# Four edits at once in a two-layer attention and ConvFFN kernel: the input stage, two waits filled with products, a shorter norm step, and the second attention's outputs split ahead of the sample

## The reference, cut to what matters

```python
h = rms_norm(x, norm1)
a_q, a_k, a_v, b_q, b_k, b_v, i_q, i_k, i_w = split_cols(h @ w_in, PROJ_SPLITS)
b_q = rms_norm(b_q.reshape(B, T, N_HEADS_B, HEAD_DIM), q_norm)
b_k = rms_norm(b_k.reshape(B, T, N_HEADS_B, HEAD_DIM), k_norm)
o_a = stick_breaking(a_q, ka, va, q_pos, k_pos)
# B: every query takes the top_k keys by an indexer's score, bias by T5 bucket, softmax
o_b = indexed_sparse_attention(b_q, kb, vb, i_q, ki, i_w, q_pos, k_pos, rel_bias, top_k)
x = x + jnp.concatenate([o_a, o_b], axis=-1) @ w_out
f, conv_new = conv_ffn(rms_norm(x, norm2), conv_state, w_up, conv_w, conv_b, w_down)
return x + f, new_rows + (conv_new,)
```

## Time and profile before

| | us |
|---|---|
| median of three runs | 1620.74 |
| the profiled execution's own time | 1622.25 |
| its span, first to last instruction | 1620.5 |
| PE busy | 1551.6 (96%) |
| DVE busy | 928.3 (57%) |
| ACT busy | 684.6 (42%) |
| POOL busy | 628.4 (39%) |
| mean granted TensorE clock | 0.991 |

### The profile page before, as it was taken

The page is one execution under the profiler, slowest core; times in us unless marked ns, Lnnn a source line. Parts: engine busy times, 40 slices in busy tenths (PEclk is TensorE's granted clock), DMA queues, the critical chain, the costliest instruction groups (busy, mean ns, idle before and its releaser), DMA issues.

```text
span 1620.5 us, 29945 instructions
## 1 busy us (share of the span) xinstructions
PE 1551.6 (96%) x11838; PEld 1443.5 (89%) x11838; DVE 928.3 (57%) x1721; ACT 684.6 (42%) x1302; POOL 628.4 (39%) x346
## 2 busy tenths in 40 slices
PE   6999999989999999999999999998899999999998
PEld 5788887759999999999987898876699999999998
DVE  6666666746566156426757666666466642662461
ACT  4425564554444144224433355455434432442342
POOL 5223232326543433434542333232374434434332
PEclk9999999999999999999999999999999999999999
DMA  4444321112323223223242422211132332332323
GB/s 134 134 126 134 85 75 39 57 58 66 91 79 92 85 86 92 82 89 89 76 115 82 117 75 77 66 44 43 61 92 79 92 92 79 92 92 79 91 79 97
DMA packets 246338, 138.19 MB, mean 85 GB/s; under 512 B 11006, under 2 KB 239214, under 8 KB 246198
## 3 DMA queue, kind: packets, MB, share of 16 engines
q1 hardware_dynamic: 246198, 136.28, 29.0%
HBM read 121.19 MB, written 14.24 MB: 84 GB/s over the span
## 4 chain that ended last, share of the span: by engine, by line
PE 79%; DVE 10%; ACT 4%; issue 2%; POOL 2%; DVEq 2%; ACTq 1%; DMA 0%; SPq 0%
PE g_ps L1224 15%; PE g_ps L1225 14%; PE g_ps L1228 14%; PE a_ps L1225 8%; PE a_ps L1224 8%; PE a_ps L1228 8%; PE a_ps L709 2%; DVE prob L1697 1%; PE a_ps L1322 1%; PE a_ps L1303 1%; POOL w_lo L1721 1%; PE a_ps L1349 1%; DVE score L1639 1%; ACT w_hi L940 1%; PE a_ps L1416 1%
## 5 line engine op out<-in xcount | busy, mean ns | idle before, releaser
L1721 POOL TENSOR_TENSOR w_lo<-raw,w_hi 128x1024 fp32r<-128x1024 f32 (+2 forms) x210 | 504.3, 2402 | 698.5 <-ACT w_hi L940 698.4
L1224 PE MATMUL g_ps<-h_hi,w_hi 128*128 128x272 f32 (+1 forms) x1616 | 449.9, 296 | 10.2 <-DVEq L1598 4.1
L1225 PE MATMUL g_ps<-h_lo,w_hi 128*128 128x272 f32 (+1 forms) x1616 | 439.6, 290 | 0.0
L940 ACT ACTIVATE w_hi<-raw 128x1024 fp32r<-128x1024 f32 (+2 forms) x210 | 217.5, 1036 | 457.2 <-PE g_ps L1228 317.9
L1228 PE MATMUL g_ps<-h_hi,w_lo 128*128 128x272 f32 (+1 forms) x1616 | 337.3, 290 | 0.0
L1224 PEld LDWEIGHTS g_ps<-h_hi,w_hi 128*128 128x128 f32 (+1 forms) x1616 | 306.2, 189 | 25.0 <-issue 9.1
L1225 PEld LDWEIGHTS g_ps<-h_lo,w_hi 128*128 128x128 f32 (+1 forms) x1616 | 306.0, 189 | 0.6
L1607 DVE SCALAR_TENSOR_TENSOR wts<-work,par,wts 128x546 f32<-128x546 f32 x176 | 202.6, 1151 | 99.6 <-ACT wts L1122 92.2
L1228 PEld LDWEIGHTS g_ps<-h_hi,w_lo 128*128 128x128 f32 (+1 forms) x1616 | 254.4, 189 | 0.0
L1224 PE MATMUL a_ps<-h_hi,w_hi 128*128 128x272 f32 x720 | 194.9, 288 | 0.0
L1225 PE MATMUL a_ps<-h_lo,w_hi 128*128 128x272 f32 x720 | 194.4, 288 | 0.0
(11 more groups left out here) (233 smaller groups left out, 2718.8 us busy)
## 6 DMA issues: line engine op xcount, KB each, us to landing
raw<-in_w_up SPq DMA_DIRECT2D x88, 512.0 KB, 3.7
raw<-in_w_in SPq DMA_DIRECT2D x56, 512.0 KB, 3.6
raw<-in_w_down SPq DMA_DIRECT2D x32, 512.0 KB, 3.8
raw<-in_w_out SPq DMA_DIRECT2D x16, 512.0 KB, 3.8
raw<-in_w_down SPq DMA_DIRECT2D x16, 384.0 KB, 3.4
strip<-bias_turns SPq DMA_DIRECT2D x12, 256.0 KB, 3.5
bias_turns<-bias_line SPq DMA_DIRECT2D x8, 320.0 KB, 5.2
x_nat<-in_x_prompt SPq DMA_DIRECT2D x4, 512.0 KB, 5.7
```

Source lines behind the costliest of these rows:

```text
L940: act.activation(w_hi[:, n % SPLIT, 0:kt, 0:c], raw[:, n % RAW, 0:kt, 0:c], ACT.Copy).then_inc(hi_done, 1)
L1224: pe.matmul(g[0:c, a, 0:HALF], w_hi[:, s, j, 0:c], xh[:, mov], start=(j == 0), stop=False)
L1225: pe.matmul(g[0:c, a, 0:HALF], w_hi[:, s, j, 0:c], xl[:, mov], start=False, stop=False)
L1721: pool.tensor_tensor(w_lo[:, s, 0:kt, 0:c], raw[:, n % RAW, 0:kt, 0:c], w_hi[:, s, 0:kt, 0:c].bitcast(F32), ALU.subtract).then_inc(lo_done, 1)
```

## The change

1. **Input stage.** x is loaded by four DMAs issued from ACT's queue at the start; SP loads only identity and ones, the sample's x and the gains before the weights, and the tables and masks later. PE starts when the identity and the sample's x are there. The squares of the eight tiles are made by ACT (new step "SX", L1014) in PSUM and added by DVE. R moves between the halves of ("iq", 0), the bias line between the halves of ("iq", 1).
2. **Products in two waits.** Fourteen bf16 products of 240 columns before the sums N of ("bk", 1), 24 before BL of pair j = 12. They go to columns of a PSUM bank that nothing reads.
3. **Norm step.** ACT squares y after making it (`va` = y^2). DVE has three operations: raw * gain * y, (total + n*eps) * y^2, and (that - 3n) * the first, with constants folded into the gain.
4. **Outputs of attention B.** Tiles 4 to 7 are split for the prompt's 512 columns (steps "OP") as soon as each is there, into a new buffer `qk_hi`; the sample's 32 columns of all four in one step "OS". PE makes the prompt side (columns 0 to 271) of these tiles in steps "WP", three matmuls each, some ahead of the sample's product. The weights of wo 2 and wo 3 are split in two parts, the first (step "C1") before the sample.

```diff
+    half[last + 4] += [("G", "wo", 1, 0)] + [("OP", j) for j in range(KT // 2, KT - 1)]
+    after[last + 4] += [("C1", "wo", 2), ("C1", "wo", 3), ("WP", 0, KT // 2), ("WP", 0, KT // 2 + 1)]
...
-    s += [("BV", "s")]
+    s += [("WP", 0, KT - 2), ("OP", KT - 1), ("BV", "s"), ("OS",), ("WP", 0, KT - 1)] + [("WP", 1, j) for j in range(KT // 2, KT // 2 + 2)]
...
-    s += product("iq", 0) + norm if l == 0 else norm + product("iq", 0)
-    s += [("E", "iq", 0)] + product("iq", 1) + [("E", "iq", 1), ("kci",), ("LK", "a"), ("T", "ik", 0), ("IDX", 0, 0)]
+    first, second = product("iq", 0), product("iq", 1)
+    if l == 0:
+        s += [first[0]] + norm + [first[1]]
+        second = [second[0], ("line",), second[1]]
+    else:
+        s += norm + first
+    s += [("E", "iq", 0)] + second + [("E", "iq", 1), ("kci",), ("LK", "a"), ("T", "ik", 0), ("IDX", 0, 0)]
...
-    s += [("O", j) for j in range(KT // 2, KT)]
-    s += [("G", "wo", 0, 1), ("E", "wo", 0), ("X", 2, 0), ("G", "wo", 1, 1), ("E", "wo", 1), ("X", 2, 1)]
+    s += [("G", "wo", 0, 1), ("E", "wo", 0), ("X", 2, 0)] + [("WP", 1, j) for j in range(KT // 2 + 2, KT)] + [("G", "wo", 1, 1), ("E", "wo", 1), ("X", 2, 1)]
...
-    out += [(0, ("L", 2)), (0, ("C", 1)), (0, ("L", 3))]
+    out += [(0, ("C", 1))] + [(0, ("SX", j)) for j in range(KT)]
+    out += [(0, ("L", 2)), (0, ("L", 3))]
...
+        def idle_products(pe, bank, n):
+
+            for _ in range(n):
+                pe.matmul(bank[:, HALF:512], ident_b, cb[:].rearrange("p a b -> p (a b)")[:, 0:512 - HALF], start=False, stop=False, skip_group_check=True)
...
         def _(act):
-            act.wait_ge(pro_in, 112)
...
+            for i in range(X_CHUNKS):
+                cols = slice(i * DM // X_CHUNKS, (i + 1) * DM // X_CHUNKS)
+                act.dma_start(x_nat[:, :, cols], io["x_prompt"][0].rearrange("(t p) d -> p t d", p=P)[:, :, cols]).then_inc(pro_x[i], 16)
...
+                elif k == "C1":
+                    n = l * NU + unit_no[st[1:]]
+                    act.wait_ge(loaded[n % RAW], loaded_at(n))
+                    act.wait_ge(wo_half.sem, wo_half.at(l, st[2] - SPLIT))
+                    act.activation(w_part(w_hi, SPLIT, n, True), w_part(raw, RAW, n, True), ACT.Copy).then_inc(hi_half.sem, 1)
...
+                elif k == "SX":
+
+                    j = st[1]
+                    if j < 2:
+                        act.wait_ge(pro_free, KT)
+                    else:
+                        act.wait_ge(sqx_added, j - 1)
+                    part = halves(sq[:, 1, :]) if j == 0 else a_pair[j % 2][:, :, 0:HALF]
+                    act.activation(part, halves(x_t[:, j, :]), ACT.Square).then_inc(sqx_part, 1)
...
                     act.activation(vb[:], vb[:], ACT.Exp, scale=-0.5).then_inc(y_done.sem, 1)
+                    if st[1] != "R":
+                        act.drain()
+                        act.activation(va[:], vb[:], ACT.Square)
+                        act.drain()
+                    act.sem_inc(yy_done.sem, 1)
...
+                elif k == "OP":
+                    j = st[1]
+                    act.wait_ge(o_out.sem, o_out.at(l, ("b", j - PAIRS)))
+                    act.wait_ge(bl_full.sem, bl_full.at(l, (NH - 1, QB - 1)))
+                    act.activation(o_high(j)[:, 0:SEQ], o_t[:, j, 0:SEQ], ACT.Copy).then_inc(op_hi.sem, 1)
+                elif k == "OS":
+                    act.wait_ge(o_out.sem, o_out.at(l, ("b", "s")))
+                    act.activation(qk_hi[:, :, SEQ:TOK], o_smp(o_t), ACT.Copy).then_inc(os_hi.sem, 1)
...
         def _(pe):
-            pe.wait_ge(pro_in, 112)
...
+            pe.wait_ge(pro_ident, 32)
...
-                    if st[3] == 0:
+                    if st[3] == 0 and (kind, i) in halved:
+                        pe.wait_ge(lo_half.sem, lo_half.at(l, (kind, i)))
+                    elif st[3] == 0 or (kind, i) in halved:
                         pe.wait_ge(lo_done, l * NU + n + 1)
+                    early = kind == "wo" and i < 2
+                    if early and st[3] == 1:
+                        pe.wait_ge(os_split.sem, os_split.at(l, "s"))
...
+                        sides = (1,) if early and st[3] == 1 else (0, 1)
...
+                elif k == "WP":
+
+                    i, j = st[1], st[2]
+                    s = (l * NU + unit_no[("wo", i)]) % SPLIT
+                    z = gslot(l, ("G", "wo", i))[:, 0, 0:HALF]
+                    xh, xl = o_high(j)[:, 0:HALF], act_hi[:, j, 0:HALF]
+                    pe.wait_ge(op_split.sem, op_split.at(l, j))
+                    pe.matmul(z, w_hi[:, s, j, 0:P], xh, start=False, stop=False)
+                    pe.matmul(z, w_hi[:, s, j, 0:P], xl, start=False, stop=False)
+                    pe.matmul(z, w_lo[:, s, j, 0:P], xh, start=False, stop=(j == KT - 1))
...
                 elif k == "N":
+                    if st[1:] == ("bk", 1):
+                        idle_products(pe, g[:, 0, :], 14)
...
                     else:
+                        if pair[0] == (NH - 2, 0):
+                            idle_products(pe, gslot(l, ("G", "bv", PAIRS - 1))[:, 0, :], 24)
                         pe.wait_ge(b_max.sem, b_max.at(l, btiles[2 * j - 1]))
...
-                        for i in ([j] if j < EARLY else range(EARLY, KT) if j == KT - 1 else []):
-                            squares(dve, i)
...
+                elif k == "SX":
+                    j = st[1]
+                    dve.wait_ge(sqx_part, j + 1)
+                    if j:
+                        dve.tensor_tensor(halves(sq[:, 1, :]), halves(sq[:, 1, :]), a_pair[j % 2][:, :, 0:HALF], ALU.add)
...
+                        gain = qk_gain[:, 0:1] if st[1] == "bq" else qk_gain[:, 1:2]
+                        dve.scalar_tensor_tensor(norm_raw(st[1]), norm_raw(st[1]), gain, vb[:], ALU.mult, ALU.mult)
+                        dve.wait_ge(yy_done.sem, yy_done.at(l, st[1:]))
+                        dve.scalar_tensor_tensor(halves(va[:]), total_of(l, st[1:]), n * EPS, halves(va[:]), ALU.add, ALU.mult)
+                        dve.drain()
+                        dve.sem_inc(v_done.sem, 1)
                         freed(dve, l, ("N", *st[1:]))
...
-                        dve.scalar_tensor_tensor(k_t[:, k_slot("bk", p), :], norm_raw("bk"), qk_gain[:, 1:2], vb[:], ALU.mult, ALU.mult)
+                        dve.scalar_tensor_tensor(k_t[:, k_slot("bk", p), :], va[:], -3.0 * HD, norm_raw("bk"), ALU.add, ALU.mult)
```

159 lines of the change are left out of this document (101 added, 58 removed).

## The result

The changed kernel takes 1592.01 us (median of four runs, 1589.77 to 1593.36), the kernel before in the same session 1621.14 (1618.93 to 1622.55). The ratio is 0.982, 95% interval 0.9803 to 0.9837: 29.1 us faster. The profiled execution took 1593.36 with a span of 1591.6. A later session with five runs of the same program gave 1591.98 and a ratio of 0.9822 (0.9809 to 0.9836). The forecast was 1594.3 in a range of 1588 to 1603. All ratios are of runs at a mean clock of 0.988 or more; one run of the kernel "Only the norm step" took 1880.27 us at a mean clock of 0.752 and is left out.

The account below looks back on a forecast made before the run. PE, busy for 96% of the span, was taken as the bound. Gains of 6.6 + 2.9 + 0.2 + 6.9 + 12.7 = 29.3 us, less 2.9 put back, net 26.4, took 1620.74 to 1594.3 us, range 1588 to 1603.

Parts of the forecast that it names:

- Input stage: From the start to the first IDX: IDX at 41.9 instead of 48.48, gain 6.6 us, bounds 2.7 to 8.4.
- the transposes start at 5.2: Start of the kernel: x loaded from ACT's empty queue about 3.4 us earlier, first transposes at 5.2 instead of 8.62.
- the path from R to IDX without a wait: Input stage: 12.2 us from R at 29.7 to IDX at 41.9, with the earlier DMA wait of 1.24 gone.
- The rule that was put down as a rival: Start: DMA engines alternate between two queues packet by packet, slowing loads; input stage gives less, 1598 us, chance 0.12.
- Norm step: Attention B norms: 0.85 us less on DVE each, 2.9 us gained in PE's waits, bounds nothing to 4.5.
- only norms with a PE wait behind them pay back: Attention B: of PE's four waits for ACT's squares, two shrink by 0.85 each and two go, 2.9 us.
- Products: Waits before ("bk", 1) and pair 12: fillers cost or gain little, 0.2 us gained, and hold the clock, 6.9 us.
- the price of a fall: Behind ("bk", 1) and pair 12: each us at 1.2 GHz taken to cost 0.45 us, together 6.9 us.
- Outputs: End of attention B, sample's product to wo 2: gains 6.85 and 5.85 us by layer, 12.7 in all, between 7.5 and 13.5.
- the clock still falls behind the sample's product: End of attention B: half clock after L720's small products costs 2.6 and 2.4 us, time 1599; chance 0.15.
- A tenth put back: Whole kernel: 2.9 us of the 29.3 returned because engines that had slack in attention B will be waited for.
- Slower and no change: Slower: clock at 1.2 GHz through attention B, about 1670 us, case 0.03; final chances slower 0.02, same 0.02.

Follow-up runs that it names:

- Only the norm step: The kernel before with the norm step of three operations as its only edit; ratio 0.9945 (0.9926 to 0.9963).
- the execution without a fall: Profiled execution of the changed kernel timed again with no edit, clock never falling before PE's last product; 1591.98 us, ratio 0.9822.

## Why the prediction was right, and which terms were not

The forecast of the total, 1594.3 against 1592.0, is in part luck: terms that were off by several us cancelled. By terms:

- **Input stage, 6.6 forecast, 5.0 measured.** Two steps failed, "the transposes start at 5.2" and the path from R to IDX without a wait. The rule that was put down as a rival is what happened: with two queues in use the sample's x took 5.7 us to land. ACT's first scaling came at 9.32 instead of 7.7, and 1.2 us of this was left at 26.06 (forecast 24.9) and 0.5 at R (30.21, forecast 29.7; the wait there 0.9, not 1.8). The rest was lost at IDX, where the sum had no wait: 1.1 us, 0.7 for DVE's operation on ("iq", 1) and 0.4 for the cached keys that DVE copies behind it. Squares on ACT and adds at 0.72 us came as forecast.
- **Norm step, 2.9 forecast, 11 to 14 measured.** The time saved on DVE is nearly right (0.95 instead of 0.85 a norm). The mis-sized term is where it pays: "only norms with a PE wait behind them pay back" looked for waits of PE for ACT's squares. But DVE's later work for PE (row maxima, the next product out of PSUM) stands behind each norm in the same queue, and of the 3.5 us of wait for a row maximum in front of pair 12, which the sum left as it was, 1.7 went with the norm step alone, as did 1.3 of the 3.1 at ("bk", 1), not 0.85. The upper bound, 4.5, was too low for the same reason.
- **Products, 7.1 forecast with the clock, about nothing measured on top of the norm step.** The clock did stay up behind ("bk", 1) and pair 12. With products and the new norm step it never fell there, at 36 such places in nine profiled executions; with the new norm step and no products it fell at 5 of 12. What failed is the price of a fall, 0.45 us for each us at 1.2 GHz. It holds behind ("bk", 1), 1.5 us for 3.4; behind pair 12, 3.4 us at 1.2 GHz cost nothing and 6.8 us cost 0.9. The cost was put at up to 0.15 and 0.1 us; at 0.104 us a product they end 0.7 and 0.6 us late, which costs 0.6 at ("bk", 1) and nothing at pair 12. Left out was that fourteen products can start only when DVE frees their slot, after 0.9 of the 1.6 us of wait.
- **Both together, 10.0 forecast, 12.6 measured.** The sum came nearly right because the two errors have opposite signs. The time alone would have confirmed a wrong split.
- **Outputs, 12.7 forecast, 9.8 measured in the first profile (5.4 + 4.4).** Undoing the edit gave 10.0 over the same stretches. In the execution without a fall it is 6.9 + 5.9, the forecast's own terms. The rival "the clock still falls behind the sample's product" came true in one profiled execution and not in the other, at 1.5 us a layer, not 2.5.
- **A tenth put back, 2.9.** It failed: nothing was given back. Without it and with the fall priced at 3 us the forecast would have been 1594.4 all the same.
- **Slower and no change.** No sign of either: no stretch in attention B of the changed kernel was at 1.2 GHz.

What stays open: when a fall comes, and why 1.4 us of earlier start and 1.1 us of shorter attention B gave 1.5 us of time. Executions differ by about as much in where the clock falls, and in the pace of PE at full clock (last section).

## What to carry to other kernels

When one engine's queue carries every step of a chain, an operation saved in it pays wherever PE later waits for that engine, also where the wait names another tile; add up the savings between two waits before pricing them. Fill a wait only with what ends inside it, counted from the moment the filler itself may start. When two edits aim at one wait, run all four combinations: here they summed to nearly the right time with the wrong shares. Before pricing a lost microsecond, look for the next wait of the same engine: it may take it back.
